# VectorE transposes all of x's last 512 features at stage boundaries, and the first two chunks interleave by two steps from their fifth on

## The reference, cut to what matters

```python
x = x + rms_norm(mixer(rms_norm(x, mix_pre_g[l])), mix_post_g[l])      # l = 0, 1
x = x + rms_norm(sq_relu_mlp(rms_norm(x, ffn_pre_g[l])), ffn_post_g[l])
...
h = rms_norm(x, norm_g_2); proj = h @ w_in_2      # 11264 columns: q, k, v, gates
q, k = rms_norm per head of 128; attention; gating
x = x + merged @ w_out_2
```

## Time and profile before

| what | value |
|---|---|
| median of 3 runs | 2681.44 us |
| the profiled execution's own time | 2682.01 us |
| its span | 2680.3 us |
| TensorE busy | 2674.5 us of the span |
| VectorE busy | 1907.5 us |
| ScalarE busy | 1293.6 us |
| GpSimd busy | 288.5 us |
| mean DMA rate | 192 GB/s |

### The profile page before, as it was taken

How to read it: one execution, slowest core, us unless ns; L and a number is a source line. 1 busy time by engine, 2 the same in 40 slices (tenths; PEclk the granted TensorE clock), 3 DMA queues, 4 the chain that set the end, 5 groups by cost and what they waited for, 6 DMA issues and landing times.

```text
span 2680.3 us, 31135 instructions
## 1 busy us (share of the span) xinstructions
PE 2674.5 (100%) x11969; PEld 2215.6 (83%) x11969; DVE 1907.5 (71%) x2594; ACT 1293.6 (48%) x1635; POOL 288.5 (11%) x263
## 2 busy tenths in 40 slices
PE   9999999999999999999999999999999999999999
PEld 7888888888888888888888888888888888888887
DVE  6887867666776777776777676667668867765564
ACT  6875544444444454444544444444445546544442
POOL 4841100000000010000100000000011001000000
PEclk9999999999999999999999999999999999999999
DMA  8555665555655556555556555556555655555554
GB/s 256 188 173 190 207 200 188 189 188 191 208 185 193 201 184 206 198 194 198 179 194 205 198 189 188 189 189 205 187 188 181 209 182 174 174 201 191 188 189 157
DMA packets 268148, 515.58 MB, mean 192 GB/s; under 512 B 8498, under 2 KB 28260, under 8 KB 267492
## 3 DMA queue, kind: packets, MB, share of 16 engines
q1 hardware_dynamic: 267732, 513.34, 57.0%
q10 hardware_dynamic: 272, 0.26, 0.0%
HBM read 511.47 MB, written 2.10 MB: 192 GB/s over the span
## 4 chain that ended last, share of the span: by engine, by line
PE 99%; DMA 0%; DVE 0%; SPq 0%; DVEq 0%; issue 0%
PE bank L823 33%; PE bank L825 32%; PE bank L824 32%; PE bank L874 0%; PE bank L892 0%; PE bank L1055 0%; DMA x_res<-in_x 0%; DMA w_raw<-in_ab_w_in 0%; PE bank L1015 0%; PE bank L1069 0%; PE bank L1076 0%; PE bank L1041 0%; PE bank L1084 0%; PE bank L1085 0%; PE bank L1042 0%; PE bank L1083 0%
## 5 line engine op out<-in xcount | busy, mean ns | idle before, releaser
L802 DVE TENSOR_TENSOR w_lo<-w_raw,w_hi 128x1024 fp32r<-128x1024 f32 x950 | 1182.4, 1265 | 470.0 <-ACT w_hi L784 463.9
L784 ACT ACTIVATE w_hi<-w_raw 128x1024 fp32r<-128x1024 f32 x954 | 973.2, 1056 | 594.6 <-PE bank L825 423.6
L823 PE MATMUL bank<-w_hi,A_lo 128*128 128x512 f32 x2432 | 952.3, 392 | 0.0
L825 PE MATMUL bank<-w_hi,A_hi 128*128 128x512 f32 x2432 | 947.1, 389 | 0.0
L824 PE MATMUL bank<-w_lo,A_hi 128*128 128x512 f32 x2432 | 946.6, 389 | 0.0
L823 PE MATMUL bank<-w_hi,B_lo 128*128 128x512 f32 x1408 | 548.7, 390 | 0.0
L825 PE MATMUL bank<-w_hi,B_hi 128*128 128x512 f32 x1408 | 547.9, 389 | 0.0
L824 PE MATMUL bank<-w_lo,B_hi 128*128 128x512 f32 x1408 | 547.8, 389 | 0.0
L823 PEld LDWEIGHTS bank<-w_hi,A_lo 128*128 128x128 f32 x2432 | 456.8, 188 | 95.7 <-DVE w_lo L792 1.4
L825 PEld LDWEIGHTS bank<-w_hi,A_hi 128*128 128x128 f32 x2432 | 456.6, 188 | 95.8
L824 PEld LDWEIGHTS bank<-w_lo,A_hi 128*128 128x128 f32 x2432 | 456.8, 188 | 92.9
(11 more groups left out here) (180 smaller groups left out, 1004.6 us busy)
## 6 DMA issues: line engine op xcount, KB each, us to landing
w_raw<-in_ffn_w SPq DMA_DIRECT2D x256, 1024.0 KB, 5.2
w_raw<-in_w_in SPq DMA_DIRECT2D x88, 1024.0 KB, 5.0
w_raw<-in_sc_w_in SPq DMA_DIRECT2D x48, 1024.0 KB, 5.1
w_raw<-in_ab_w_out SPq DMA_DIRECT2D x16, 1024.0 KB, 4.9
w_raw<-in_sc_w_out SPq DMA_DIRECT2D x16, 1024.0 KB, 5.1
w_raw<-in_w_out SPq DMA_DIRECT2D x16, 1024.0 KB, 5.1
w_raw<-in_ab_w_in SPq DMA_DIRECT2D x26, 512.0 KB, 4.8
w_raw<-in_ab_w_in SPq DMA_DIRECT2D x8, 1024.0 KB, 5.2
```

The costliest lines, as they stand in the source:

```text
L784: e.activation(w_hi[:, s % SPLIT_SLOTS, :], raw_step(s), ACT.Copy).then_inc(hi_made, 1)
L802: e.tensor_tensor(w_lo[:, slot, :], raw_step(s), w_hi[:, slot, :].bitcast(F32), ALU.subtract).then_inc(lo_made, 1)
L823: e.matmul(ps, lo[:, kt, tok], wh, start=first, stop=False)
L825: ins = e.matmul(ps, hi[:, kt, tok], wh, start=False, stop=last)
```

## The change

VectorE transposes all 512 features of group 3 at the four boundaries, in 16 transposes of 32 by 256 over six steps (3 to 8), so TensorE's four transposes for it go, and `x_T` is twice as large. The first two chunks go by turns of four steps once, and then by turns of two: `(c, 0..3), (c+1, 0..3), (c, 4), (c, 5), (c+1, 4), (c+1, 5), (c, 6), (c, 7), (c+1, 6), (c+1, 7)`. Group 3 is then first read at step 12; the first chunk ends after step 13, the second after step 15 as before. ScalarE casts group 3 at step 9, VectorE at step 10. In VectorE's boundary `update(2, 0)` and `update(2, 1)` move ahead of `lo_tile(1, 1)`, and `update(3, ...)` ahead of the split of step 5. `QK_TURNS` gives the first q chunk five steps instead of six, which now begin two steps later, and the second five instead of six from one step later.

```diff
--- before.py
+++ after.py
@@ -40,6 +40,7 @@
 Z_SLOTS = 3
 TAP_SLOTS = 2
 TURN_STEPS = 8
+LAST_TURNS = 6
 STEP_K = 2
 AHEAD = 3
 SCRATCH = 1024
@@ -146,7 +147,7 @@
 
 
 
-QK_TURNS = [(3, 6), (5, 6), (3, 5), (3, 5)]
+QK_TURNS = [(3, 5), (6, 5), (3, 5), (3, 5)]
 
 
 GATED_AT = [(C_L1 + 4, 3), (C_L1 + 7, 3), (C_L1 + 10, 3), (C_L1 + 12, 2)]
@@ -234,7 +235,7 @@
     by_vector = {"h": range(2), "cu": range(NG), "bg": range(NG - 1), "qk": range(4), "ws": range(2), "ao": range(2),
                  "merged": range(NG - 1)}
     for key in turn_order():
-        if key[0] == "pre" and key[1] > 0 and key[2:] == (NG - 1, 1):
+        if key[0] == "pre" and key[1] > 0 and key[2] == NG - 1:
             continue
         if key[0] not in by_vector or key[1] not in by_vector[key[0]]:
             yield key
@@ -276,8 +277,9 @@
         for first, end in zip(STAGE[:-1], STAGE[1:]):
             rest = first
             if first > 0:
-                for half in range(2):
-                    SEQ += [(c, 4 * half + i) for c in (first, first + 1) for i in range(4)]
+                SEQ += [(c, i) for c in (first, first + 1) for i in range(4)]
+                for half in range(2, 4):
+                    SEQ += [(c, 2 * half + i) for c in (first, first + 1) for i in range(2)]
                 rest = first + 2
             while rest < end:
                 if rest in (6, 10):
@@ -356,7 +358,7 @@
         side_T = [v.rearrange("p (k t) -> p k t", k=GK) for v in (conv_in_flat[:, 0:GK * TOK], conv_in_flat[:, GK * TOK:2 * GK * TOK],
                                                                     conv_out_flat[:, 0:GK * TOK])]
         qk_squares = conv_in_flat[:, 0:NT * CH].rearrange("p (t c) -> p t c", t=NT)
-        x_T = conv_out_flat[:, GK * TOK:(GK + 2) * TOK].rearrange("p (k t) -> p k t", k=2)
+        x_T = conv_out_flat[:, GK * TOK:2 * GK * TOK].rearrange("p (k t) -> p k t", k=GK)
         ws_T = ws_flat.rearrange("p (g c) -> p g c", g=HEADS)
         scores = scores_flat.rearrange("p (s c) -> p s c", s=2)
         probs_T = prod_rows
@@ -864,9 +866,9 @@
                     e.wait_ge(sem, value)
                 return aux_bank(*key)
 
-            def turn(src, *key, parts=two):
-
-                for h in parts:
+            def turn(src, *key):
+
+                for h in two:
                     view = aux_begin(*key, h).rearrange("p (k t) -> p k t", k=2)
                     for k in two:
                         for tt in tiles:
@@ -879,8 +881,7 @@
                     e.wait_ge(x_loaded[g], 16)
                 else:
                     e.wait_ge(x_made.sem, x_made.of(p - 1, g, 1))
-                turn(lambda tt, f: x[:, tt, g * CH + f.start:g * CH + f.stop], "pre", p, g,
-                     parts=range(1) if p > 0 and g == NG - 1 else two)
+                turn(lambda tt, f: x[:, tt, g * CH + f.start:g * CH + f.stop], "pre", p, g)
 
             def turn_tile(p, g, tt):
 
@@ -989,8 +990,8 @@
 
             for c, i in matmul_steps(e, 2):
                 j, part = divmod(c - C_L1, 3)
-                if c == C_L1 + 1 and i in (0, 2):
-                    turn_x(2, 2 + i // 2)
+                if (c, i) == (C_L1 + 1, 0):
+                    turn_x(2, 2)
                 if (c, i) == (C_L1 + 12, 1):
                     e.wait_ge(act_took.sem, act_took.of(c - 1, 1))
                     turn_z(z_slot("b", NG - 1), "bg", NG - 1)
@@ -1002,8 +1003,8 @@
 
             for c, i in matmul_steps(e, 4):
                 r = c - C_L2
-                if r == 1 and i in (0, 2):
-                    turn_x(4, 2 + i // 2)
+                if (r, i) == (1, 0):
+                    turn_x(4, 2)
                 if (r, i) in ((11, 1), (13, 1)):
                     j = (r - 11) // 2
                     e.wait_ge(ws_turned.sem, ws_turned.of())
@@ -1059,8 +1060,8 @@
         def pe_mlp(e, turn_x, layer):
             p = 1 + 2 * layer
             for c, i in matmul_steps(e, p):
-                if c == up_chunk(layer, 0, 1) and i in (0, 2):
-                    turn_x(p, 2 + i // 2)
+                if (c, i) == (up_chunk(layer, 0, 1), 0):
+                    turn_x(p, 2)
 
         def pe_attention(e, aux_begin, task, h):
             if task == "scores":
@@ -1122,10 +1123,11 @@
             def hi_turned(p):
 
                 e.wait_ge(x_turned.sem, x_turned.of(p))
-                for k in two:
-                    kt = GK * NG - 2 + k
-                    ins = e.activation(halves["A"][0][:, kt, :], x_T[:, k, :], ACT.Copy, scale=par_col(PRE_COL[p], kt))
-                ins.then_inc(hi_cast("pre", p, NG - 1, 1), 1)
+                for h in two:
+                    for k in (2 * h, 2 * h + 1):
+                        kt = GK * (NG - 1) + k
+                        ins = e.activation(halves["A"][0][:, kt, :], x_T[:, k, :], ACT.Copy, scale=par_col(PRE_COL[p], kt))
+                    ins.then_inc(hi_cast("pre", p, NG - 1, h), 1)
 
             def hi_tile(p, g, tt):
 
@@ -1194,9 +1196,7 @@
                     hi_x(p, 2)
                 if (c, i) == (STAGE[p] + 1, 1):
                     statistics(p)
-                if (c, i) == (STAGE[p] + 1, 2):
-                    hi_half(p, NG - 1, 0)
-                if (c, i) == (STAGE[p], 4):
+                if (c, i) == (STAGE[p], 5):
                     hi_turned(p)
 
 
@@ -1523,23 +1523,23 @@
 
                 if n == 0:
                     e.wait_ge(x_made.sem, x_made.of(p - 1, NG - 1, 1))
-                tok = slice(32 * n, 32 * n + 32)
-                for q in range(4):
-                    feat = slice(32 * q, 32 * q + 32)
+                for m in range(16 * n // LAST_TURNS, 16 * (n + 1) // LAST_TURNS):
+                    tok, feat = (slice(32 * q, 32 * q + 32) for q in divmod(m, 4))
                     ins = e.transpose(x_T[feat, :, :].rearrange("p k (t c) -> p t k c", t=NT)[:, :, :, tok],
-                                      x[tok, :, D - CH // 2:].rearrange("p t (k c) -> p t k c", k=2)[:, :, :, feat])
-                if n == 3:
+                                      x[tok, :, D - CH:].rearrange("p t (k c) -> p t k c", k=GK)[:, :, :, feat])
+                if n == LAST_TURNS - 1:
                     ins.then_inc(x_turned(p), 1)
 
             def lo_turned(p):
 
                 hi, lo = halves["A"]
-                e.wait_ge(hi_cast.sem, hi_cast.of("pre", p, NG - 1, 1))
-                for k in two:
-                    kt = GK * NG - 2 + k
-                    ins = e.scalar_tensor_tensor(lo[:, kt, :], x_T[:, k, :], par_col(PRE_COL[p], kt),
-                                                 hi[:, kt, :].bitcast(F32), ALU.mult, ALU.subtract)
-                ins.then_inc(lo_cast("pre", p, NG - 1, 1), 1)
+                for h in two:
+                    e.wait_ge(hi_cast.sem, hi_cast.of("pre", p, NG - 1, h))
+                    for k in (2 * h, 2 * h + 1):
+                        kt = GK * (NG - 1) + k
+                        ins = e.scalar_tensor_tensor(lo[:, kt, :], x_T[:, k, :], par_col(PRE_COL[p], kt),
+                                                     hi[:, kt, :].bitcast(F32), ALU.mult, ALU.subtract)
+                    ins.then_inc(lo_cast("pre", p, NG - 1, h), 1)
 
             def lo_part(p, g, tt, h):
 
@@ -1634,21 +1634,21 @@
                 split_to(e, split_lo, at, f + 3)
                 lo_tile(p, 0, 1)
                 update(p - 1, 1, 1)
+                for tt in tiles:
+                    update(p - 1, 2, tt)
                 lo_tile(p, 1, 1)
-                for g in (2, 3):
-                    split_to(e, split_lo, at, f + 2 + g)
-                    for tt in tiles:
-                        update(p - 1, g, tt)
+                split_to(e, split_lo, at, f + 4)
+                for tt in tiles:
+                    update(p - 1, 3, tt)
+                split_to(e, split_lo, at, f + 5)
 
             def early(p, c, i):
                 if (c, i) == (STAGE[p] + 1, 0):
                     lo_x(p, 2)
                 n = POS[c, i] - S0[STAGE[p]] - 3
-                if 0 <= n < 4:
+                if 0 <= n < LAST_TURNS:
                     turn_last(p, n)
-                if (c, i) == (STAGE[p] + 1, 2):
-                    lo_half(p, NG - 1, 0)
-                if (c, i) == (STAGE[p] + 1, 3):
+                if (c, i) == (STAGE[p] + 1, 4):
                     lo_turned(p)
                 if (c, i) == (STAGE[p], 4):
                     statistics(p)
```

## The result

The changed kernel takes 2684.88 us (median of 22 runs, 2684.5 to 2685.84) against 2681.48 us of the kernel before (22 runs, 2680.73 to 2682.19): 3.4 us more, a ratio of 1.0013 with a 95% interval of 1.0007 to 1.0019. That is slower by less than 0.2%, so "the same" by the bound set above, and 1.0 us under the prediction of 2685.9. The profiled execution took 2684.89 us, with a span of 2683.2.

A forecast was written before the change was run, and what follows sets the result against it. TensorE's work, plus any wait the change brings, was taken as the bound. Per boundary -0.49 + 0.77 + 0.35 = +0.63, four times +2.5, plus +1.9 in the last layer: +4.4 us, 2685.9 us; range 2681.4 to 2687.8.

The forecast's parts named there:

- Part 1: At each of four boundaries TensorE loses four transposes, all of which counts: -0.49 us each, -2.0 us in all.
- Part 2: At each boundary GpSimd's gain blocks the second update, so lo_tile(1, 1) starts late: +0.77 us each, +3.1 us in all.
- Part 3: At each boundary wider transposes and a later cast make TensorE wait at step 12: +0.35 us, +1.4 us in all.
- rule of thumb: TensorE's late weight loads: 0.10 us of a load's lateness is absorbed, since loads run ahead of matmuls.
- Part 4: Last layer's q and k: VectorE falls behind, TensorE waits at steps 28 and 30, about +1.9 us.
- list of signs: For the last layer: VectorE busy without a gap, steps 16 to 35; TensorE gaps at 28 and 30 near 0.5 and 1.4 us.
- Part 5: MLPs and mixer: later hidden-result transposes and casts still meet TensorE's need, 0.7 us spare in an MLP; cost nothing.
- Rival C: Step 34 of both MLPs: late casts of the second hidden result make TensorE wait, +1.6 us, 2687.4 us; chance 0.12.
- A: Boundaries: GpSimd's gain and VectorE's updates run side by side without a port effect, 2682.8 us; chance 0.24.
- B: Boundaries and last layer: VectorE's idle time covers all waits, only the -2.0 us stays, 2679.5 us; chance 0.06.
- D: Steps 8 to 11: weight loads hold up the new order of steps and TensorE waits; chance 0.03, either side.

The follow-up runs named there:

- experiment 5: Changed kernel with three edits: GpSimd's last gain waits for update(2, 1), lo_turned at step 9, q and k transposes spread over more steps; 2679.7 us, 0.9992 of before.
- 8: The kernel of experiment 5 with four of group 2's TensorE transposes done twice at each boundary; 2681.33 us, 0.9999 of the kernel before.
- 9: The kernel of experiment 5 unchanged, timed again beside 8 on the same chip; 2679.99 us, 0.9993 of the kernel before.
- experiment 2: Changed kernel with GpSimd's last gain multiplication waiting for update(2, 1) instead of update(1, 1); 2682.42 us, 1.0004 of the kernel before.
- experiment 3: Changed kernel with VectorE's casts of group 3 (lo_turned) at step 9, ahead of the split of step 13; 2684.12 us, 1.0009 of the kernel before.
- experiment 4: Changed kernel with QK_TURNS = [(3, 7), (8, 5), (5, 7), (4, 5)], spreading the last layer's transposes; 2683.24 us, 1.0006 of the kernel before.
- experiment 7: Changed kernel with ScalarE's scaling of the first q result one step later, behind the third chunk's eviction; measured once, 2684.54 us.
- experiment 6: The kernel before with only the new order of updates in VectorE's boundary; 2684.68 us, 1.0011 of the kernel before.
- experiment 1: Changed kernel with update(2, 0) and update(2, 1) back behind lo_tile(1, 1); 2685.0 us, 1.0013 of the kernel before.

## Why the prediction was right

Every term had the right sign and mechanism. The sizes of parts 2 to 4 all came out too dear, by 0.15 and 0.09 us a boundary (0.6 and 0.4 us over four) and by 0.3 us in the last layer, so the total was not right by errors that cancel. The range, 6.4 us wide, is no sharp test of this; the rows are. The terms, against what the runs give:

```
part                          predicted     measured    from
1  four transposes go         -0.49 x4      -0.48 x4    stretch, before and experiment 5 (8 against 9: -0.38 x4)
2  updates against the gain   +0.77 x4      +0.62 x4    experiment 2 (stretch; medians 2.46 in all)
3  wait ahead of step 12      +0.35 x4      +0.26 x4    experiment 3 (stretch; medians 0.76 in all)
4  q and k of the last layer  +1.9          +1.6        experiment 4 (medians)
5  MLPs and mixer              0             0          no wait there
sum                           +4.4          +3.2        medians of the kernels: +3.4
```

**Part 1** held. It was read from one gap in the earlier trace rows, and it shows where nothing else is late, in experiment 5. Experiments 8 and 9, which change nothing but four transposes, give 1.3 to 1.5 us for what the prediction had as 2.0; the difference may lie in their place, in a row of eight.

**Part 2** had the right mechanism and was 0.15 us too dear. The prediction let GpSimd begin when the first update ends and the second update let go 2.47 us after the first began; measured it is 2.37 (253.68 to 256.05). The gain of 1.29 us ends at 255.57 (253.84 + 1.73), so it got going at about 254.28, 0.60 us after the update that held it began, not 0.66; and VectorE's next instruction starts 0.48 us after the gain ends, for which I had 0.5 (256.3 to 256.81). That is 0.1 of the 0.15; the other 0.05 lies between VectorE (+0.66, 3.03 less 2.37) and TensorE (+0.62), and I have no row for it. The second update took 1.78 us, not 1.9. Its behaviour is what the pairs of the earlier trace rows show: the gain waits behind the first update, goes ahead of the second, and that one is blocked until it is nearly through. The Trainium skill (SBUF — State Buffer, Who interferes with whom) has it that such a pair of instructions excludes each other and that the order of issue decides who waits; the 1.73 and 1.78 us here agree, and the 2.07 us of three updates in experiment 2 shows the other side.

**Part 3** was laid out through 26 us of VectorE's queue and came out within 0.1: the idle before VectorE's split was to be 1.5 us (measured 1.40), and that split to start at 280.41 (measured 280.33). The starts compare because two shifts cancel: the prediction's stand without part 2 (VectorE +0.66), and this profile began 0.63 us earlier (254.66 for 255.29). The wait itself, 0.26 for 0.35, is the measure. The load idles 0.44 us for a predicted 0.46, but more of it is absorbed than the rule of thumb had: TensorE's matmuls ahead of and behind this load start at 282.06, 282.50 and 282.81, 0.75 us for two starts instead of 0.45, so 0.29 is lost and 0.15 absorbed, not 0.10.

**Part 4** named both steps. The waits were to be near 0.5 and 1.4; they are 0.35 and 1.54. VectorE is about as late as forecast: its splits of step 16 and step 30 are

```profile
2051.41 1.22 DVE L804 TENSOR_TENSOR w_lo<-w_raw,w_hi 128x1024 fp32r<-128x1024 f32 x1 [1.75 <-ACT w_hi L786]
...
2086.07 1.22 DVE L804 TENSOR_TENSOR w_lo<-w_raw,w_hi 128x1024 fp32r<-128x1024 f32 x1
```

which is 34.66 us apart, against 32.61 in the earlier trace rows (2050.25 to 2082.86): 2.05 more, where the prediction had 2.2. In between it idles once, 0.51 us before its split at 2075.23 (in the kernel before once too, 0.31 us at 2067.72). The prediction's sum allowed 0.1 us more of such waiting, while its list of signs said none. That idle time is ScalarE's, whose scaling of the first q result stands ahead of its split; without it (experiment 7) the wait at step 28 goes. The term was 0.3 too dear chiefly because it took the 0.10 us of absorbed lateness once, while two loads are late and each absorbs more, as TensorE's matmuls around them show:

```profile
2080.14 0.39 PE L827 MATMUL bank<-w_hi,A_hi 128*128 128x512 f32 x1
2080.45 0.50 PE L825 MATMUL bank<-w_hi,A_lo 128*128 128x512 f32 x1
2080.79 0.40 PE L826 MATMUL bank<-w_lo,A_hi 128*128 128x512 f32 x1
...
2085.84 0.39 PE L827 MATMUL bank<-w_hi,A_hi 128*128 128x512 f32 x1
2087.34 0.50 PE L825 MATMUL bank<-w_hi,A_lo 128*128 128x512 f32 x1 [1.12 <-DVE w_lo L804]
2087.69 0.40 PE L826 MATMUL bank<-w_lo,A_hi 128*128 128x512 f32 x1
```

Two starts take 0.45 us undisturbed. Here they take 0.65 and 1.85, so 0.2 and 1.4 us are lost for idle times of 0.35 and 1.54: 0.3 us absorbed, and a cost of 1.6, as experiment 4 measured.

**Part 5**: no wait at step 34 of an MLP. VectorE's timeline of the first one at the split of 35 and the cast after it:

```profile
339.52 1.64 DVE L804 TENSOR_TENSOR w_lo<-w_raw,w_hi 128x1024 fp32r<-128x1024 f32 x1 [3.02 <-ACT w_hi L786]
341.08 1.28 DVE L1974 TENSOR_TENSOR B_lo<-conv_out,B_hi 128x512 fp32r<-128x512 f32 x2
```

VectorE idles 3.02 us before this split, so it has room to spare; the split takes 1.64 instead of 1.22, beside GpSimd's squares, and still nothing waits. Rival C is out.

**The rivals.** A (2682.8) is what experiment 2 makes, 2682.42, by moving GpSimd instead of supposing that it doesn't matter. B (2679.5) is experiment 5, 2679.7: without the three waits the kernel is 1.7 us under the one before. Neither is the change as made. D is out: TensorE waits nowhere between steps 4 and 12.

**What is left.** The terms give 3.2 us, the medians 3.4, and the profiles from the first boundary's load to the end 3.5. The start of the kernel scatters by 1.4 us between executions, and one profile against another can't settle 0.2 or 0.3.

A version that beats the changed kernel is experiment 5, by about 5 us: 3.4 over the kernel before against 1.7 under it, the latter in two series on two chips (0.9992 and 0.9993), but both intervals include 1, and it is less than the 0.2% named above: not shown to be faster, though its trace shows 1.9 us of work gone and nothing in its place.

## What to carry to other kernels

Work of VectorE that reads two SBUF tensors was not free in VectorE's idle time, because GpSimd read SBUF just then: look up what GpSimd does in such a gap, and if it is in the way, move its start (one wait changed here, worth 2.5 us) before you give up the gap. When a queue is laid out anew, look for an instruction that itself waits and stands ahead of one that doesn't; and where a wait is removed by postponing work, read the next deadlines before counting the gain, since in experiment 1 all of it came back in the steps behind.

## What the runs showed of the hardware

- The form of the updates, `scalar_tensor_tensor` with two tensors from SBUF, is blocked by a GpSimd `tensor_tensor` as a VectorE `tensor_tensor` is: 1.78 us for 0.74. None of the earlier trace rows showed it. The casts of the MLP, `tensor_tensor` of two SBUF tensors, suffer too: beside GpSimd's squares two of them take 2.13 us instead of 1.28, in VectorE's and GpSimd's timelines of the changed kernel:

```profile
317.33 2.13 DVE L1974 TENSOR_TENSOR B_lo<-conv_out,B_hi 128x512 fp32r<-128x512 f32 x2 [4.57 <-ACT B_hi L1460]
```

```profile
316.28 2.04 POOL L2227 TENSOR_TENSOR z<-z 128x512 f32<-128x512 f32 x2 [19.72 <-ACT z L1101]
```

- A waiting GpSimd instruction goes ahead of VectorE's next one even if that one comes without a gap: this was the doubtful step of part 2, and it held at all four boundaries, in the changed kernel and in that of experiment 6 (the longest gain at each takes 1.73, the longest update 1.77 to 1.78).
- The price of both engines' overlap isn't the sum of their times: the three updates and the gain, 2.07 and 1.29 us alone, take 3.10 us from the start of the first update to the end of the last.
- The start of the kernel varies by 1.4 us between executions of nearly the same code, with the waits for the first inputs and splits (0.3 to 1.4 us for x, and in experiment 2's profile 1.0 us for a split at 28.41); a difference under some 1 us between two profiles needs a stretch that leaves it out.
